# The second mixer's lanes ordered separately for each engine, and the head outputs split straight from PSUM

## The reference, cut to what matters

```python
def second_block(x, c, ctx, ...):
    ...
    h = _rmsnorm(x, norm1_w[i]) * (1.0 + mod[:, 1]) + mod[:, 0]
    x_out, _ = _token_mixer(h, w_in[i], ..., ctx_states, rope)
    x = x + mod[:, 2] * x_out
    h2 = _rmsnorm(x, norm2_w[i]) * (1.0 + mod[:, 4]) + mod[:, 3]
    x = x + mod[:, 5] * _expert_choice_ffn(h2, w_router[i], w_exp_gate[i], w_exp_up[i], w_exp_down[i])
    ...

def _token_mixer(h, w_in, ...):
    gq, gk, gv, log_a, gg, rq, rk, rv, rg = _project(h, w_in, gla_gate_w, gla_gate_b, rope)   # rotary step on rq, rk
    o_gf, s_gf = _gla_chunked(gq, gk, gv, log_a[:, :, 0], s_gf)          # gated linear attention, forward
    o_gb, s_gb = _gla_chunked(_flip(gq), _flip(gk), _flip(gv), ...)      # and backward
    o_rf, s_rf = _retention_chunked(rq, rk, rv, log_gamma[0], s_rf)
    o_rb, s_rb = _retention_chunked(_flip(rq), _flip(rk), _flip(rv), log_gamma[1], s_rb)
    o_g = _head_rmsnorm(o_gf + _flip(o_gb), gla_norm_w) * jax.nn.silu(gg)
    o_r = _head_layernorm(o_rf + _flip(o_rb), ret_norm_w) * jax.nn.silu(rg)
    out = jnp.concatenate([o_g, o_r], axis=-1) @ w_out
    ...
```

## Time and profile before

| | |
|---|---|
| median of 3 runs | 1363.94 us (1363.89 to 1365.08) |
| profiled execution | 1366.02 us, its span 1364.2 us |
| PE / DVE / ACT busy share of the span | 74% / 39% / 21% |
| bytes moved by DMA | 415.16 MB, mean 304 GB/s |

### The profile page before, as it was taken

The page is one execution under the profiler, slowest core; times in us unless marked ns, Lnnn a source line. Parts: engine busy times, 40 slices in busy tenths (PEclk is TensorE's granted clock), DMA queues, the critical chain, the costliest instruction groups (busy, mean ns, idle before and its releaser), DMA issues.

```text
span 1364.2 us, 13077 instructions
## 1 busy us (share of the span) xinstructions
PE 1015.9 (74%) x5454; PEld 587.7 (43%) x5454; DVE 527.0 (39%) x1001; ACT 290.9 (21%) x465; POOL 25.4 (2%) x38
## 2 busy tenths in 40 slices
PE   1797888899989998999987866555555655566594
PEld 0575667777675786777864311111111111111131
DVE  6876667686553498577674100000000000000001
ACT  3322244452241333551332100000000000000000
POOL 0000000000000000000000000000000000000000
PEclk9997788899989999899987866777787788877878
DMA  9896211567634468232359999999999999999996
GB/s 387 329 376 242 95 62 62 193 253 275 249 120 154 157 253 343 79 135 89 115 209 420 425 429 431 431 431 428 432 430 430 431 428 432 431 430 431 429 431 264
DMA packets 41147, 415.16 MB, mean 304 GB/s; under 512 B 4928, under 2 KB 4928, under 8 KB 7808
## 3 DMA queue, kind: packets, MB, share of 16 engines
q1 hardware_dynamic: 38304, 405.75, 72.6%
q10 hardware_dynamic: 2784, 8.57, 1.7%
HBM read 413.26 MB, written 1.05 MB: 304 GB/s over the span
## 4 chain that ended last, share of the span: by engine, by line
PE 42%; DMA 41%; DVE 12%; ACT 3%; issue 2%; POOL 1%; DVEq 0%; SPq 0%
DMA ring<-in_w_egu 26%; DMA ring<-in_w_ed 10%; PE PS L656 7%; PE PS L657 7%; PE PS L658 7%; PE PS L957 4%; PE PS L1274 3%; DVE ringR L1490 2%; DMA arena<-in_w_ed 2%; PE PS L565 2%; PE PS L1336 2%; DMA ring<-in_w_in 1%; DVE arena L1367 1%; ACT ringR L2404 1%; DVE ring L1409 1%
## 5 line engine op out<-in xcount | busy, mean ns | idle before, releaser
L1274 PE MATMUL PS<-ring,arena 128*32 128x512 f32 (+1 forms) x1152 | 179.9, 761 | 100.0 <-DMA ring<-in_w_egu 99.7
L656 PE MATMUL PS<-ringR,arenaR 128*128 128x512 f32 (+1 forms) x520 | 215.2, 414 | 24.0 <-DVE arenaR L1478 23.5
L657 PE MATMUL PS<-ringR,arenaR 128*128 128x512 f32 (+1 forms) x520 | 207.4, 399 | 0.0
L658 PE MATMUL PS<-ringR,arenaR 128*128 128x512 f32 (+1 forms) x520 | 207.2, 398 | 0.0
L1490 DVE TENSOR_TENSOR ringR<-ring,ringR 128x2048 fp32r<-128x2048 f32 (+1 forms) x66 | 148.7, 2254 | 98.7 <-ACT ringR L2404 98.6
L1367 DVE SCALAR_TENSOR_TENSOR arena<-arena,PS 128x256 f32<-128x256 f32 (+2 forms) x68 | 33.2, 498 | 368.0 <-ACT arena L2837 360.9
L2404 ACT ACTIVATE ringR<-ring 128x2048 fp32r<-128x2048 f32 (+1 forms) x66 | 123.9, 1885 | 88.7 <-PE PS L658 54.0
L1274 PEld LDWEIGHTS PS<-ring,arena 128*32 128x32 f32 x1152 | 36.8, 131 | 233.4 <-DMA ring<-in_w_egu 171.2
L1336 PE MATMUL PS<-ring,arena 128*32 128x512 f32 x512 | 82.9, 782 | 59.5 <-DMA ring<-in_w_ed 58.9
L656 PEld LDWEIGHTS PS<-ringR,arenaR 128*128 128x128 f32 x520 | 99.5, 191 | 51.0 <-DVE arenaR L1478 24.4
L2837 ACT ACTIVATE arena<-PS 128x512 f32<-128x512 f32 (+1 forms) x12 | 6.7, 561 | 503.0 <-PE PS L1274 503.0
(11 more groups left out here) (344 smaller groups left out, 887.9 us busy)
## 6 DMA issues: line engine op xcount, KB each, us to landing
ring<-in_w_egu SPq DMA_DIRECT2D x48, 2048.0 KB, 35.5
ring<-in_w_ed SPq DMA_DIRECT2D x32, 2048.0 KB, 34.4
ring<-in_w_vad SPq DMA_DIRECT2D x40, 1024.0 KB, 7.0
ring<-in_w_egu SPq DMA_DIRECT2D x24, 1536.0 KB, 29.6
arena<-in_w_egu SPq DMA_DIRECT2D x16, 2048.0 KB, 35.2
ring<-in_w_in SPq DMA_DIRECT2D x22, 1024.0 KB, 4.8
ring<-in_w_gu SPq DMA_DIRECT2D x22, 1024.0 KB, 4.9
arena<-in_w_ed SPq DMA_DIRECT2D x11, 2048.0 KB, 32.5
```

The lines of the kernel that those rows point to most:

```text
L656: mm(o, xh(k, t), hi[:, c], start=k == 0, stop=False)
L657: mm(o, xh(k, t), s.viewr[:, c], start=False, stop=False)
L658: i = mm(o, xl(k, t), hi[:, c], start=False, stop=k == nk - 1)
L1274: i = mm(PS[32 * ee:32 * ee + 32, b + a_, 0:fw], XEv[:, k, grp, 32 * ee:32 * ee + 32], wv[:, ee, a_, :], start=k == 0, stop=k == 7, tile_p ...
```

## The change

The one string `GLA` becomes three, `MIX_PE`, `MIX_DVE` and `MIX_ACT`, and copying out a column group of `in2` becomes a lane `e` of its own on VectorE and ScalarE. The rotary step on VectorE is cut in two (one for each token tile) and stands behind the first and the second masking instead of ahead of both. On TensorE the transposes of the rotated queries and keys move one slot back, the product with the values and the first state update move behind slot 8 and ahead of those transposes, each retention head moves by about one slot, and GLA OT stands ahead of slot 13 instead of behind it. The heads are split straight from PSUM: ScalarE writes the high part (`a out2 xh`) and VectorE subtracts it from PSUM (`rest_of`). RET OT stands behind slot 1 of `out2` instead of behind slot 0.

```diff
-GLA = "w g w g d w g d w g g w g g w r g w g w r g w g r w g r w g r w g r t w g r g r g w g r t r".split()
+MIX_PE = ("w g w g w g w g g w g g w r g w g w w g g r w g r w g r w g g r w r g g g r w r r r").split()
...
             hh2 = [tile(rnd(HH5)), tile(rnd(HH6))]
             for n, _ in enumerate(dense("out2", lambda k, t: hh2[k // 4](k % 4, t), tile(rnd(hT2)), lambda g, t: 4 * t + g,
-                                        lambda g, t: [at("v gla ot"), at("a gla ot")])):
-                if n == 0:
+                                        lambda g, t: [at("v out2 xl", 1)])):
+                if n == 1:
                     next(lanes["r"])
...
+            def rest_of(S, j, x, hi, lo):
+
+                w.wait_ge(*at(f"a {S} xh", j))
+                tt(lo, x, hi, ALU.subtract).then_inc(*sig(f"v {S} xl", j))
...
-                    g = group_end("in2", n)
-                    if g is not None:
-                        c0, wc = G_IN2[g]
-                        w.wait_ge(*out_ready("in2", g, 1))
-                        cp(pjv[:, 1, c0:c0 + wc], PS[:, 7, 0:wc]).then_inc(*sig("v in2 ev", g))
+                    yield
+
+            def out_in2():
+                for g, (c0, wc) in enumerate(G_IN2):
+                    w.wait_ge(*out_ready("in2", g, 1))
+                    cp(pjv[:, 1, c0:c0 + wc], PS[:, 7, 0:wc]).then_inc(*sig("v in2 ev", g))
                     yield
...
-                w.wait_ge(*at("pe gla ot", 0))
-                cp(hT2[:, 0:512], PS[:, 0, :]).then_inc(*sig("v gla ot"))
                 for j in range(2):
-                    if j:
-                        w.wait_ge(*at("a gla ot"))
-                    halves("out2", j, rnd(HH5)[:, 512 * j:512 * j + 512], pieces(hT2, 512 * j))
-                low("out2", 2)
+                    rest_of("out2", j, PS[:, j, :], rnd(HH5)[:, 512 * j:512 * j + 512], rnd(hT2)[:, 512 * j:512 * j + 512])
...
-                w.wait_ge(*at("pe ret ot", 0))
-                cp(hT2[:, 1024:1536], PS[:, 3, :]).then_inc(*sig("v ret ot"))
-                for j in range(2, 4):
-                    if j > 2:
-                        w.wait_ge(*at("a ret ot"))
-                    halves("out2", j, rnd(HH6)[:, 512 * j - 1024:512 * j - 512], pieces(hT2, 512 * j))
-                yield
+                for j, b in ((2, 3), (3, 6)):
+                    rest_of("out2", j, PS[:, b, :], rnd(HH6)[:, 512 * j - 1024:512 * j - 512], rnd(hT2)[:, 512 * j:512 * j + 512])
+                yield
...
-                w.wait_ge(*at("pe gla ot", 1))
-                act(hT2[:, 512:1024], PS[:, 1, :], ACT.Copy).then_inc(*sig("a gla ot"))
+                for j in range(2):
+                    w.wait_ge(*at("pe gla ot", j))
+                    act(rnd(HH5)[:, 512 * j:512 * j + 512], PS[:, j, :], ACT.Copy).then_inc(*sig("a out2 xh", j))
```

More of the change, by code:

```diff
@@ L87 @@
 ATT, FFN = schedules()
-GLA = "w g w g d w g d w g g w g g w r g w g w r g w g r w g r w g r w g r t w g r g r g w g r t r".split()
+MIX_PE = ("w g w g w g w g g w g g w r g w g w w g g r w g r w g r w g g r w r g g g r w r r r").split()
+MIX_DVE = ("w g w e g d w g d w e g g w g g w e g w r g w e r w g g r w e g r w g r w e g g t r g w g r r g r e r w t r").split()
+MIX_ACT = ("w g w e g d w g d w e g g w g g w e r g w g w e w g g r w e g r w g r w e g t g r w r w g g g r e r t").split()
 LATE = ("Mf", "Mb", "mskf", "mskb", "Rp", "Rm", "cosR", "sinR", "H4")
@@ L1207, in tensor @@
             lanes = {"w": w_in2(), "g": gla(), "r": retention()}
-            for k in GLA:
-                if k in lanes:
-                    next(lanes[k])
+            for k in MIX_PE:
+                next(lanes[k])
             hh2 = [tile(rnd(HH5)), tile(rnd(HH6))]
             for n, _ in enumerate(dense("out2", lambda k, t: hh2[k // 4](k % 4, t), tile(rnd(hT2)), lambda g, t: 4 * t + g,
-                                        lambda g, t: [at("v gla ot"), at("a gla ot")])):
-                if n == 0:
+                                        lambda g, t: [at("v out2 xl", 1)])):
+                if n == 1:
                     next(lanes["r"])
@@ L2154, in gla @@
                 cp(OG[:, 0, :], PS[:, 4, :]).then_inc(*sig("v gla og"))
-                w.wait_ge(*at("pe rt bias"))
-                cp(BT, PS[:, 0, 0:16]).then_inc(*sig("v rt bias"))
                 yield
@@ L2159, in gla @@
                 yield
+                w.wait_ge(*at("pe rt bias"))
+                cp(BT, PS[:, 0, 0:16]).then_inc(*sig("v rt bias"))
                 head_norm("gla", 0, OG, 1056)
                 yield
-                w.wait_ge(*at("pe gla ot", 0))
-                cp(hT2[:, 0:512], PS[:, 0, :]).then_inc(*sig("v gla ot"))
                 for j in range(2):
-                    if j:
-                        w.wait_ge(*at("a gla ot"))
-                    halves("out2", j, rnd(HH5)[:, 512 * j:512 * j + 512], pieces(hT2, 512 * j))
-                low("out2", 2)
+                    rest_of("out2", j, PS[:, j, :], rnd(HH5)[:, 512 * j:512 * j + 512], rnd(hT2)[:, 512 * j:512 * j + 512])
                 yield
@@ L2223, in retention @@
                 yield
-                w.wait_ge(*at("pe ret ot", 0))
-                cp(hT2[:, 1024:1536], PS[:, 3, :]).then_inc(*sig("v ret ot"))
-                for j in range(2, 4):
-                    if j > 2:
-                        w.wait_ge(*at("a ret ot"))
-                    halves("out2", j, rnd(HH6)[:, 512 * j - 1024:512 * j - 512], pieces(hT2, 512 * j))
+                for j, b in ((2, 3), (3, 6)):
+                    rest_of("out2", j, PS[:, b, :], rnd(HH6)[:, 512 * j - 1024:512 * j - 512], rnd(hT2)[:, 512 * j:512 * j + 512])
                 yield
-            lanes = {"w": w_in2(), "g": gla(), "r": retention(), "d": decays(), "t": gates()}
-            for k in GLA:
+            lanes = {"w": w_in2(), "e": out_in2(), "g": gla(), "r": retention(), "d": decays(), "t": gates()}
+            for k in MIX_DVE:
                 next(lanes[k])
+            low("out2", 2)
             next(lanes["r"])
@@ L2690, in w_in2, with out_in2 @@
                         top_half("out2", n - 12)
[L2691 to L2695, removed]
                     if n == 2:
                         gate_row(2, 4, mods2[:, 0:1024])
+                    yield
+            def out_in2():
+                for g, (c0, wc) in enumerate(G_IN2):
+                    w.wait_ge(*out_ready("in2", g, 0))
+                    act(pjv[:, 0, c0:c0 + wc], PS[:, 2, 0:wc], ACT.Copy).then_inc(*sig("a in2 ev", g))
                     yield
@@ L2777, in retention @@
                 yield
-                w.wait_ge(*at("pe ret ot", 1))
-                act(hT2[:, 1536:2048], PS[:, 6, :], ACT.Copy).then_inc(*sig("a ret ot"))
+                for j, b in ((2, 3), (3, 6)):
+                    w.wait_ge(*at("pe ret ot", j - 2))
+                    act(rnd(HH6)[:, 512 * j - 1024:512 * j - 512], PS[:, b, :], ACT.Copy).then_inc(*sig("a out2 xh", j))
                 yield
-            lanes = {"w": w_in2(), "g": gla(), "r": retention(), "d": decays(), "t": gates()}
-            for k in GLA:
+            lanes = {"w": w_in2(), "e": out_in2(), "g": gla(), "r": retention(), "d": decays(), "t": gates()}
+            for k in MIX_ACT:
                 next(lanes[k])
             top_half("out2", 2)
-            next(lanes["r"])
             top_half("out2", 3)
+            for _ in range(3):
+                next(lanes["r"])
             gate_row(3, 2, mods2[:, 1024:2048])
```

## The result

The median after is 1353.77 us (1352.80 to 1354.61, 5 runs), that of before 1364.16 us in the runs on the same chip. The ratio is 0.9918, with a 95% interval from 0.9903 to 0.9933: 0.8% faster, where 1354.1 us was predicted. A second set on another chip gave 1353.65 us and a ratio of 0.9927 (0.9912 to 0.9942). The profiled execution took 1352.8 us, its span is 1351.0 us. Single executions of several kernels lie 7 to 18 us above their median (of the kernel before 1372.69 us here); they are counted in the medians, and the trace of experiment 4 is of such a one (1363.58 us).

The account below looks back on a forecast made before the run. The prediction took the expert-weight stream, started by RET OT, as the bound. 16.3 − 5.6 − 1.8 = 8.9 us earlier, plus 0.9 for the closed pause, is 9.8 us off 1363.9: 1354.1 us, range 1353 to 1355.5 (chance 0.55).

Parts of the forecast that it names:

- The bound: End of the run: a 276.8 MB stream of expert weights at 431 GB/s, which starts when RET OT is done.
- The sum: TensorE ahead of RET OT: 16.3 us of waits removed, less 5.6 and 1.8 added, so RET OT 8.9 us earlier.
- The second scores, 7.1 us: TensorE, slot 6 to slot 7: waiting for the masking (5.2 us) and lower clock behind it (1.6 and 0.3) go.
- The new wait, 1.8 us: TensorE idles between the two halves of the transposes for VectorE's copy: 1.8 us, bounds 0 and 4.4.
- Rival 1: Smaller gain: clock falls behind the new wait and slot 9 runs slower, 2.6 us back, 1356.7 us; chance 0.15.
- GLA OT and the split, 6.7 us: TensorE from GLA OT through slot 0 of `out2`: 4.1 us waiting for split heads and 2.6 us of lower clock go.
- Margins: VectorE's results ready before TensorE needs them: 2.2 us early at RET OT, 1.2 at group 3, about 1 at GLA OT.
- Behind RET OT: TensorE waits 1 to 1.5 us for the split after RET OT, and reaches the router 13.3 us earlier.
- The pause: Expert stream at the ninth load, which waits for `gate_up(0, 0, 0)`: the 0.9 us lost there closes.
- Fewer instructions on VectorE: VectorE: eight instructions fewer, hidden, with their effect counted in the waits.

Follow-up runs that it names:

- experiment 4: Kernel after with the old splitting of the heads (copied out, then split by `halves`), so the three orders alone: 1354.02 us, ratio 0.9931 to the kernel before.
- 1: Kernel after with the mixer's four scratch places given to the expert loads after slot 2 of `out2`, not after RET OT: 1361.89 us.
- 2: Kernel after with the first expert load's place released when the last retention head's products are done, not after RET OT: 1350.26 us.
- Experiment 7: Kernel after with the transposes of queries and keys back right behind slot 7, their copies right behind the rotary step: 1361.88 us.
- 9: Kernel after with GLA OT, its two copies and two subtractions back behind slot 13, RET OT staying behind slot 1: 1357.15 us.
- 3: Kernel before with only the heads split straight from PSUM, in the one old order: 1364.76 us, ratio 1.0010.
- 11: Repeat of the kernel after with the first expert load's place released early, timed beside the unchanged kernel after: 1351.31 us.
- 12: Repeat of the kernel after with both the early first load and the transposes ahead of the first state update: 1350.93 us.
- 6: Kernel after with the transposes of queries and keys ahead of the first state update on TensorE and VectorE: 1354.37 us.
- 8: Kernel after with both the early first load and the transposes ahead of the first state update: 1351.88 us.

## Why the prediction was right, point by point

- **The bound.** The stream's start sets the end: shown by 1 (later start, later end) and 2 (earlier start, earlier end), with TensorE's order unchanged in both.
- **The sum.** 8.9 us ahead of RET OT were predicted, 9.0 measured (95.68 less 86.70, first scores to RET OT). With the 2.6 us by which this execution was ahead, RET OT was due at 690.4 - 2.6 = 687.8 and came at 687.71.
- **The second scores, 7.1 us.** No idle time, full clock, slot 7 in 5.65 us (610.16 on). Right. Experiment 7 adds what the text didn't price: without the transposes' move the wait would have been 6.0 us at another place.
- **The new wait, 1.8 us.** 1.63, and the clock stayed full: slot 9's first product takes 0.48 us. Rival 1 fell. By the rule of the Trainium skill's page TensorE: Matmul & The Clock Gate, section Part 4: PE-mode transpose, the prediction would have had 4.4 us here; the trace has 1.63 between two groups of eight transposes, and no loss of clock behind them.
- **GLA OT and the split, 6.7 us.** The waits went as predicted. But the term was put down to the place of GLA OT alone, and 9 shows that with the old place only 2.7 us come back. That the size of this term came out is luck: the other 4.0 us hang on something that the prediction didn't name. A part of it is VectorE's order. In 3, with the old order, it subtracts 3.0 us behind the start of GLA OT, since a `low` of 2.29 us stands ahead; in 9, with the new one, 1.3 us behind (677.54 to 678.80), and slot 0 runs at full clock. The experiments don't divide it further: no run has the old order of VectorE with the rest of the change.
- **Margins.** The retention's head norm was over at 685.6, 2.1 us ahead of RET OT (2.2 predicted). Group 3's copy ran from 616.76 to 617.44, 1.2 us ahead of slot 8's second tile at 615.8 + 2.8 = 618.6 (1.2 predicted). At GLA OT I was wrong: I gave 1 us, and VectorE's row ends where TensorE's begins (668.18 and 668.23), so that this place came out without a wait by luck. The head norm waited 1.80 us for GpSimd, which I had left out:

```profile
665.99 2.19 DVE L1368 SCALAR_TENSOR_TENSOR arena<-arena 128x128 f32<-128x128 f32 x8 [1.80 <-POOL arena L2862]
```

- **Behind RET OT.** 1.06 us of waiting (1 to 1.5 predicted). The ninth load was issued at 724.26, 16.0 us earlier than before, 13.4 without the 2.6 (13.3 predicted). The pause closed: no stretch from 695 to 745 us is under 423 GB/s.
- **The size that was off.** From RET OT to the end 0.9 us of gain were predicted, 1.6 measured. 0.8 is the pause: 40 us behind the start of the stream (695 to 735 us, before 705 to 745) moved 429 GB/s on average instead of 420. The other 0.8 I can put to no place, and they are not shown to be the change's: two traces of one kernel (2 and 11) differ by 1.7 us on this way (660.7 and 659.0). Total 10.6 us by the traces, 10.4 by the medians, 9.8 predicted.
- **Fewer instructions on VectorE.** The prediction says eight. They are six, 1001 before and 995 after: of each of the two groups of five, two are left. They were costed at nothing; 3 and 4 agree.

## What to carry to other kernels

When a run ends in a stream of weights at its full rate, find the instruction that releases its first transfer and add up only the waits of the bound engine ahead of it; but look at once for the next release that the same engine holds (here the ninth load): in 12 the stream began 1.2 us earlier and that release came 0.1 us earlier, and no gain could be shown. A step that is put ahead on one engine pushes another back, and the engine that waits for that one must be given other work at the same place: changed alone, the masking's move only carried the wait to the transposes, and the cheaper split carried its wait to RET OT. And count from a common mark inside the two traces: an offset of 2.6 us from work ahead of the change was a quarter of the effect.

## What the runs showed of the chip that I had not expected

- The granted clock stayed at 1.00 (2.4 GHz) behind waits of 1.06, 1.63 and 1.67 us, and products ran at the lower level (1.2 GHz) behind 3.35, 3.41 and 6.04 us. Near 2.5 us it was one or the other: behind 2.58 us full, behind 2.52 us low (RET OT in 3: 1.91 us for eight transposes instead of 1.04). The length of the wait alone doesn't decide: behind the 1.69 us that follow the router's small products in the kernel after, the clock is at 0.50 (710.37 to 711 us).
- It can also fall while TensorE doesn't wait. The same 32 router products (16 columns each) behind the same wait of 0.20 us took 3.65 us in the kernel after and 4.23 us in 6, where the clock of that stretch was 0.76:

```profile
705.00:710.00 5.00, 3.96 (x31) 3.85 (x30) 2.01 (x9) 2.88 (x6) 0.87 (x2) 0.76 0.99 423
```

The kernel after has 1.00 in the same stretch. The longest is 9, with 4.73 us: there TensorE is busy from 708.8 to 712.8 us without a gap, and the clock goes from 1.00 to 0.68 (710.8 to 711.8) and 0.50. What lies behind it I can't say. The three executions with the transposes ahead (6, 8 and 12) have 4.19 to 4.26 us, 9 has 4.73, and all others 3.64 or 3.65. In 6 and 9 no pause at the ninth load follows from it; in 8 and 12 it is half of what the transposes lost.
